# A Fourier stage on operands split in high and low parts, and attention loads on three semaphores

## The chip, the cores and the metric

The kernel runs on one core of a Trainium2 chip (the program uses no other). The metric is the time of the whole program on the device in microseconds (us), the median of several executions. The engines that compute are TensorE (PE in the rows; its weight loads are shown apart as PEld), VectorE (DVE), ScalarE (ACT) and GpSimd (POOL). SyncE (SP, its sequencer SPq) issues the DMAs.

## The reference

Two transformer-like layers follow each other on T = 2048 tokens of 1024 features. The first has five branches (spatial gating, forgetting attention, mLSTM, RWKV-7, attention over a memory of 256 tokens). The second has a Fourier branch and a neighbourhood attention. What the change touches:

```python
def _fourier(u, w_four):                      # u: 2048 x 512, four groups of 128 channels
    ug = u.reshape(b, l, F_GROUPS, F_GROUP_DIM)
    y = jnp.real(jnp.fft.fft2(ug, axes=(1, 3))) * ((l * F_GROUP_DIM) ** -0.5)
    return y.reshape(b, l, F_WIDTH) @ w_four

def forgetting_attention / memory_attention / _neighbourhood_attention:
    s = q @ k^T (+ decay or bias);  p = softmax(s);  o = p @ v
```

## The kernel before

The program is a row of phases; a barrier of all engines ends each. All tensors are float32. Most matrix products use operands kept as two `F32R` parts, high (the value rounded) and low (what the rounding left), and add three passes: high by high, high by low, low by high (`PASSES`). The Fourier phase is an exception: its matmuls take plain float32 operands.

**The Fourier phase** (`fourier`, between the feature pass 2 and the neighbourhood attention). The input `u` (4 blocks of 128 channels by 2049 columns) comes with five DMAs. The product of the channel transform `ch` and the weights `w4` gives `wcs` (8 products of 128x128 by 128x512, lines 2282, 2330, 2350). VectorE folds `u` by its symmetries into `fold[a % 2]`, four kinds `f` for each of four token blocks `a` (lines 2366 to 2381: eight operations a block). TensorE multiplies: 16 results of 4 products each (line 2294), which ScalarE (f = 0, 1) and VectorE (f = 2, 3) copy to `zz`. Two small results follow (`middle_row`, line 2300; `first_row`, lines 2307 and 2308). Then come 8 output groups `i`: 4 products for the cosines (line 2316), for the first four groups one more with a single row (`turns`, line 2319), 4 for the sines (line 2322). The tables `cs[i % 2]`, 512 KB a group, are loaded by SP (line 2247). ScalarE copies the sines out of PSUM (line 2344), VectorE forms their difference and sum with the cosines (2404, 2405), SP stores both (2262, 2265). All orders are written out by hand, engine by engine; table i + 2 is loaded when the sines of group i are done:

```python
            def load(i):
                if i >= 2:
                    sp.wait_ge(sin_ready, i - 1)
                sp.dma_start(cs[i % 2][:]..., d["dft_tokens"][i]).then_inc(cs_in[i % 2], 16)
```

**The attentions** (`attention`, used by `fox_attention`, `mem_attention` and `neighbourhood`). For each head, TensorE first computes units (line 1301: scores of a block of queries, of which VectorE takes the largest), then steps of `scores` (lines 1329 to 1337) and, two steps later, `values` (line 1346). The rows of a head come by `load_head` with 10, 7 or 11 DMAs, all counted on one semaphore `head_in`, for which TensorE waits once, before the head's first unit. `run_together` mixes the order of an attention with that of another stage by due times: `fox_attention` with the mLSTM (tiles `heads_...`), `mem_attention` with the RWKV factors (`mem_...`, `cells_...`), the neighbourhood attention (`nbr_...`) with the staging of the output weights. On each engine that order is fixed. POOL prepares constants (`const_ready`, line 1268) before the fox attention's first TensorE instruction (line 1496).

## Time and profile before

| what | value |
|---|---|
| median of 3 runs | 3731.46 us (3725.37 to 3754.88) |
| the profiled execution: time, span of its trace | 3737.91 us, 3736.2 us |
| mean granted TensorE clock, share of full speed | 0.914 |
| busy: PE, PEld, DVE, ACT, POOL | 87%, 67%, 39%, 24%, 21% |
| TensorE instructions of the span | 14595 matmuls, as many weight loads |
| Fourier phase in the trace | from 2963.2 us to about 3115 us |

A busy share is taken over the whole span, and the modelled ends of matmuls overlap, so that TensorE's speed is read from the starts of its instructions. A float32 product is two MATMUL rows in the trace, a pass on `F32R` operands one. Each phase has its own limit; what a change is worth is read where it lies.

### The profile page before, as it was taken

How to read it: one execution, taken by the hardware profiler on the slowest of the kernel's cores; microseconds unless marked ns; L12 is line 12 of the kernel's file. 1: busy time of each engine (PE TensorE's matmuls, PEld its weight loads, DVE VectorE, ACT ScalarE, POOL GpSimd, SP SyncE). 2: the span in 40 equal slices, each digit the busy share in tenths (PEclk: the TensorE clock that was granted, in tenths of full speed). 3: DMA queues.
4: the chain of work that ended last, by engine and by line, in shares of the span. 5: the costliest groups of instructions: out<-in, count | busy, mean ns of one | idle time of the engine just before them, and what ended most of it. 6: DMA issues, size and time to landing. Idle time of an engine off the chain costs nothing. (4 is left out here: it accounts for less than half of the span.)

```text
span 3736.2 us, 40044 instructions
## 1 busy us (share of the span) xinstructions
PE 3256.7 (87%) x14595; PEld 2496.7 (67%) x14595; DVE 1464.2 (39%) x2536; ACT 881.1 (24%) x1433; POOL 786.3 (21%) x843
## 2 busy tenths in 40 slices
PE   4949999899996988865699499799999895999799
PEld 2727888688885666543499388677888633666587
DVE  0023333313312667567544022277200122777533
ACT  1022221211011333342122133332001101544400
POOL 2043222211111212144333322111111001000121
PEclk7679999899997999966699699899999997999899
DMA  5333232412226134033100466522222217666364
GB/s 171 115 124 108 86 102 85 166 67 72 72 75 145 46 78 111 19 97 82 34 10 12 133 185 186 176 79 112 83 86 78 91 40 156 129 152 140 84 193 146
DMA packets 312454, 385.39 MB, mean 103 GB/s; under 512 B 86407, under 2 KB 244216, under 8 KB 297720
## 3 DMA queue, kind: packets, MB, share of 16 engines
q1 hardware_dynamic: 296276, 379.33, 35.5%
q10 hardware_dynamic: 16016, 3.95, 0.6%
q8 instruction: 95, 1.56, 0.2%
q14 instruction: 67, 0.55, 0.1%
HBM read 247.56 MB, written 135.66 MB: 103 GB/s over the span
## 5 line engine op out<-in xcount | busy, mean ns | idle before, releaser
L611 PE MATMUL f_psum_out<-f_x_high,f_w_high 128*128 128x512 f32 x1440 | 567.5, 394 | 33.3 <-DVE f_x_low L594 24.2
L611 PE MATMUL f_psum_out<-f_x_low,f_w_high 128*128 128x512 f32 x1440 | 563.2, 391 | 0.0
L611 PE MATMUL f_psum_out<-f_x_high,f_w_low 128*128 128x512 f32 x1440 | 562.8, 391 | 0.0
L611 PEld LDWEIGHTS f_psum_out<-f_x_high,f_w_high 128*128 128x128 f32 x1440 | 272.1, 189 | 94.0 <-issue 19.4
L611 PEld LDWEIGHTS f_psum_out<-f_x_low,f_w_high 128*128 128x128 f32 x1440 | 272.2, 189 | 57.4 <-issue 1.7
L611 PEld LDWEIGHTS f_psum_out<-f_x_high,f_w_low 128*128 128x128 f32 x1440 | 272.0, 189 | 57.2
L1346 PE MATMUL nbr_psum_o<-nbr_probT,nbr_v 128*128 128x512 f32 (+3 forms) x576 | 236.4, 491 | 0.3 <-ACT nbr_probT L1397 0.3
L481 PE MATMUL p_psum_proj<-p_w_high,p_h_high 128*128 128x512 f32 x512 | 208.3, 407 | 19.4 <-POOL p_w_low L296 10.5
L602 POOL CAST f_w_high<-f_w 128x1024 fp32r<-128x1024 f32 x45 | 46.7, 1039 | 768.3 <-PE f_psum_out L611 552.3
L481 PE MATMUL p_psum_proj<-p_w_low,p_h_high 128*128 128x512 f32 x512 | 202.5, 395 | 0.0
L481 PE MATMUL p_psum_proj<-p_w_high,p_h_low 128*128 128x512 f32 x512 | 202.1, 395 | 0.0
L1301 PE MATMUL nbr_psum_m<-nbr_kT,nbr_q_high 128*128 128x256 f32 (+3 forms) x352 | 158.8, 500 | 35.3 <-DMA nbr_v<-scratch_ctx_v 29.0
L1402 ACT ACTIVATE heads_probT<-heads_psum_s,heads_a_cols 128x512 f32<-128x512 f32 (+3 forms) x160 | 99.7, 623 | 276.7 <-PE heads_psum_s L1337 276.6
L1910 PE MATMUL p_psum_o<-p_w_high,p_mix_high 128*128 128x512 f32 x320 | 130.4, 408 | 26.0 <-POOL p_w_low L1979 24.8
L1346 PE MATMUL heads_psum_o<-heads_probT,heads_v 128*128 128x512 f32 (+3 forms) x320 | 148.1, 546 | 0.0
L1424 DVE CUSTOM_DVE_ANT_0 nbr_psum_m<-nbr_psum_m,nbr_inner_q 128x448 f32<-128x448 f32 x192 | 120.8, 631 | 63.9 <-PE nbr_psum_m L1301 62.9
L1397 ACT ACTIVATE nbr_probT<-nbr_probT 128x384 f32<-128x384 f32 (+2 forms) x224 | 108.6, 492 | 141.3 <-DVE nbr_probT L1440 140.5
L481 PEld LDWEIGHTS p_psum_proj<-p_w_high,p_h_high 128*128 128x128 f32 x512 | 97.8, 191 | 45.9 <-POOL p_w_low L296 12.3
L2158 DVE RECIPROCAL f_work<-f_work 128x2048 f32<-128x2048 f32 x8 | 103.6, 12952 | 62.2 <-ACT f_work L2131 62.2
L1910 PE MATMUL p_psum_o<-p_w_low,p_mix_high 128*128 128x512 f32 x320 | 127.5, 399 | 0.0
L1910 PE MATMUL p_psum_o<-p_w_high,p_mix_low 128*128 128x512 f32 x320 | 127.5, 398 | 0.0
L1301 PEld LDWEIGHTS nbr_psum_m<-nbr_kT,nbr_q_high 128*128 128x128 f32 x352 | 67.2, 196 | 81.6 <-issue 58.9
(547 smaller groups left out, 6220.5 us busy)
## 6 DMA issues: line engine op xcount, KB each, us to landing
f_w<-in_w_fm SPq DMA_DIRECT2D x45, 512.0 KB, 5.8
ada_w<-in_w_ada SPq DMA_DIRECT2D x6, 2048.0 KB, 17.6
scratch_qkmT<-p_qkT_out SPq DMA_DIRECT2D x32, 384.0 KB, 4.7
scratch_z1T<-f_out SPq DMA_DIRECT2D x10, 1024.0 KB, 4.8
p_z<-scratch_z1T SPq DMA_DIRECT2D x16, 640.0 KB, 5.8
p_xt<-in_x SPq DMA_DIRECT2D x16, 512.0 KB, 3.9
p_staging<-in_w_tok SPq DMA_DIRECT2D x8, 1024.0 KB, 5.7
scratch_hT<-p_h_slot SPq DMA_DIRECT2D x16, 512.0 KB
```

Source lines behind the costliest of these rows:

```text
L481: last = nc.tensor.matmul(p_proj[n][:], h_parts[i % 2][h_part][:, k, :], w_parts[w_part][:, k, n * BANK:(n + 1) * BANK], start=(k == 0 and ...
L602: nc.gpsimd.tensor_copy(self.w_parts[b][0][:], self.w[b][:])
L611: last = nc.tensor.matmul(self.p_out[b][:, at], self.w_parts[b][w_part][:, k, :], self.x_parts[x_part][:, k, at], start=(k == 0 and i == 0 ...
L1301: last = nc.tensor.matmul(out[:, at:at + n], query_rows(h % 2, q1[h % 2])[:, u * P:(u + 1) * P], key_rows(h % 2)[:, k:k + n], start=True, ...
L1346: nc.tensor.matmul(p_o[n % o_bufs][:, lo:hi], v[h % 2][:, b, :], probT[s % P_BUFS][:, lo:hi], start=first, stop=end).then_inc(o_ready, 1)
L1397: nc.scalar.activation(out, out, ACT.Exp).then_inc(prob_ready, 1)
L1402: nc.scalar.activation(out, p_s[s % s_bufs][:, lo:hi], ACT.Exp, bias=key_bias.column(h, b) if key_bias else 0.0).then_inc(prob_ready, 1)
L1424: last = nc.vector.tensor_tensor_reduce(scores, scores, table, 1.0, -3e38, ALU.add, ALU.max, top)
L1910: end = nc.tensor.matmul(p_o[:, n * BANK:(n + 1) * BANK], mix_parts[b][x_part][:, k, :], w_parts[w_part][:, k, n * BANK:(n + 1) * BANK], s ...
L2158: nc.vector.reciprocal(work[b][:], work[b][:])
```

## The change

Fourier phase: `wcs`, `fold`, `zz`, the tables, `middle`, `middle_row`, `turns` and `scale` become `F32R`, all but the last two in a high and a low part, and every product in the loops becomes three passes (`products`, `PASSES`); the 8 products that make `wcs` stay float32. For the splitting ScalarE now rounds (`high_of_w`, `high_of_fold`, `high_of_table`, the copies to `z_parts[0]`), and VectorE (for weights, z and the row) and POOL (for folds and tables) subtract. The split table of group i takes half of `fold[0]`; outputs and sines are placed in `u`. The reload of a raw table waits for its split. The first row of the output is computed after group 1. Attentions: the loads of a head are issued in the order of first use and counted on three semaphores, for which TensorE waits before the first unit, the first scores step and the first values step of the head.

```diff
-        def enter(h):
-            if h not in seen:
-                pe.wait_ge(head_in[h % 2], 16 * n_loads * (h // 2 + 1))
-                seen.append(h)
+        def await_loads(arrived, n, h):
+            if (n, h) not in seen:
+                pe.wait_ge(arrived[h % 2], 16 * loads[n] * (h // 2 + 1))
+                seen.append((n, h))
...
             h, q, u, pieces, masked = plan.units[plan.items[i][1]]
-            enter(h)
+            await_loads(tops_in, 0, h)
...
         def scores(s):
             h, q, b, lo, hi, first, _ = plan.steps[s]
             n, cols, out = plan.group(h, q), slice(q * BANK + lo, q * BANK + hi), p_s[s % s_bufs]
+            await_loads(scores_in, 1, h)
...
         def values(s):
             h, q, b, lo, hi, first, end = plan.steps[s]
             n = plan.group(h, q)
+            await_loads(values_in, 2, h)
...
             key_bias.load(sp, d["fox_a"])
+        sp.dma_start(raw(kx[b][0:HD, :]), d["qkmT"][0, GW + h * HD:GW + (h + 1) * HD, :]).then_inc(tops_in, 16)
+        sp.dma_start(raw(kx[b][HD:HD + 2, :]), d["fox_rows"][h]).then_inc(tops_in, 16)
+        sp.dma_start(raw(qx[b][0:HD, :]), d["qkmT"][0, h * HD:(h + 1) * HD, :]).then_inc(tops_in, 16)
         for part in range(2):
             sp.dma_start(raw(kT[b][part * HD:(part + 1) * HD, :]), d["qkmT"][part, GW + h * HD:GW + (h + 1) * HD, :])\
-                .then_inc(head_in, 16)
+                .then_inc(scores_in, 16)
             for q, half in ((q1, 0), (q2, 1)):
-                sp.dma_start(raw(q[part * HD:(part + 1) * HD, :]), d["qkmT"][half, h * HD:(h + 1) * HD, :]).then_inc(head_in, 16)
-        sp.dma_start(raw(kx[b][0:HD, :]), d["qkmT"][0, GW + h * HD:GW + (h + 1) * HD, :]).then_inc(head_in, 16)
-        sp.dma_start(raw(kx[b][HD:HD + 2, :]), d["fox_rows"][h]).then_inc(head_in, 16)
-        sp.dma_start(raw(qx[b][0:HD, :]), d["qkmT"][0, h * HD:(h + 1) * HD, :]).then_inc(head_in, 16)
+                sp.dma_start(raw(q[part * HD:(part + 1) * HD, :]), d["qkmT"][half, h * HD:(h + 1) * HD, :]).then_inc(scores_in, 16)
         sp.dma_start(v[b][:, :, b * HD:(b + 1) * HD], d["fox_v"].rearrange("(n p) c -> p n c", p=P)[:, :, h * HD:(h + 1) * HD])\
-            .then_inc(head_in, 16)
...
-    u, wcs = sb("u", [P, FK, T + 1]), sb("wcs", [P, 2, FK, D2])
...
+    u = sb("u", [P, FK, T + 1])
+    w_parts = [sb(f"w_{part}", [P, 2, FK, D2], F32R) for part in ("high", "low")]
...
-    middle, middle_row = sb("middle", [P, FK, 1]), sb("middle_row", [1, D2])
-    zz = sb("zz", [P, 4, NQ_T, D2])
-    cs = [sb(f"cs{b}", [P, NQ_T, 2, P]) for b in range(2)]
...
+    full = sb("full", [P, 4, FK, P])
+    fold = [sb(f"fold{b}", [P, 2, 4, FK, P], F32R) for b in range(2)]
...
+    row_parts = sb("row_parts", [1, 2, D2], F32R)
+    z_parts = [sb(f"z_{part}", [P, 4, NQ_T, D2], F32R) for part in ("high", "low")]
+    cs = [sb(f"cs{b}", [P, 2, NQ_T, P]) for b in range(RAWS)]
...
+    def table(i, part):
+
+        return fold[0][:, part, i % 2 * 2:i % 2 * 2 + 2]
...
             def load(i):
-                if i >= 2:
-                    sp.wait_ge(sin_ready, i - 1)
-                sp.dma_start(cs[i % 2][:].rearrange("p n s m -> p (n s m)"), d["dft_tokens"][i]).then_inc(cs_in[i % 2], 16)
-
...
+                if i >= RAWS:
+                    sp.wait_ge(table_low, i - RAWS + 1)
+                sp.dma_start(cs[i % RAWS][:].rearrange("p s n m -> p (s n m)"), d["dft_tokens"][i]).then_inc(cs_in[i % RAWS], 16)
...
+            for i in range(RAWS):
+                load(i)
...
-            sp.wait_ge(row_kept, 1)
-            sp.dma_start(d["y2"][0:1, :], first_row[:]).then_inc(row_stored, 16)
             for i, (parity, b) in enumerate(GROUPS_OUT):
-                if i + 2 < len(GROUPS_OUT):
-                    load(i + 2)
+                if i + RAWS < len(GROUPS_OUT):
+                    load(i + RAWS)
                 sp.wait_ge(out_ready, i + 1)
...
+                if i == 2:
+                    sp.wait_ge(row_kept, 1)
+                    sp.dma_start(d["y2"][0:1, :], first_row[:]).then_inc(row_stored, 16)
...
+            for n in range(HALVES):
+                a, odd = n // 2, n % 2
+                at = slice(2 * odd, 2 * odd + 2)
+                pool.wait_ge(fold_high, n + 1)
+                nc.gpsimd.tensor_tensor(fold[a % 2][:, 1, at], full[:, at], fold[a % 2][:, 0, at], ALU.subtract).then_inc(fold_low, 1)
+            for i in range(len(GROUPS_OUT)):
+                pool.wait_ge(table_high, i + 1)
+                if i >= 2:
+                    pool.wait_ge(sin_ready, i - 1)
+                nc.gpsimd.tensor_tensor(table(i, 1), cs[i % RAWS][:], table(i, 0), ALU.subtract).then_inc(table_low, 1)
...
+            over_k = [(s, m, k) for s, m in PASSES for k in range(FK)]
...
                     if f % 2 == 0:
-                        pe.wait_ge(even_ready if f == 0 else odd_ready, a + 1)
-                    if a == 0:
...
+                        pe.wait_ge(fold_low, 2 * a + f // 2 + 1)
...
-                    for k in range(FK):
-                        last = nc.tensor.matmul(p_b[a % 2 * 4 + f][:], fold[a % 2][:, f, k, :], wcs[:, f // 2, k, :],
-                                                start=(k == 0), stop=(k == FK - 1))
-                    last.then_inc(z_ready, 1)
...
+                        pe.wait_ge(z_low, 4 * (a - 2) + f + 1)
+                    products(p_b[a % 2 * 4 + f][:], over_k, lambda part, k: fold[a % 2][:, part, f, k, :],
+                             lambda part, k: w_parts[part][:, f // 2, k, :]).then_inc(z_ready, 1)
...
-                pe.wait_ge(cs_in[i % 2], 16 * (i // 2 + 1))
+                pe.wait_ge(table_low, i + 1)
...
+                if i == 0:
+                    pe.wait_ge(z_low, 4 * (NQ_T - 1) + 3)
...
+                if i == 1:
+                    pe.wait_ge(row_low, 1)
...
-                for a in range(NQ_T):
-                    last = nc.tensor.matmul(cosines[:], cs[i % 2][:, a, 0, :], zz[:, parity, a, :], start=(a == 0),
-                                            stop=(parity == 1 and a == NQ_T - 1))
+                last = products(cosines[:], over_k, lambda part, a: table(i, part)[:, 0, a, :],
+                                lambda part, a: z_parts[part][:, parity, a, :], more=parity == 0)
...
+                    for part in range(2):
+                        last = nc.tensor.matmul(cosines[:], turns[:], row_parts[:, part, :], start=False, stop=(part == 1))
...
+                products(of_sines[:], over_k, lambda part, a: table(i, part)[:, 1, a, :],
+                         lambda part, a: z_parts[part][:, 2 + parity, a, :]).then_inc(sin_ready, 1)
...
+            def high_of_w(i):
+                act.wait_ge(w_ready, i + 1)
+                for k in range(FK):
+                    nc.scalar.activation(w_parts[0][:, i, k, :], p_b[i * FK + k][:], ACT.Copy).then_inc(w_high, 1)
...
+                if a >= 2:
...
+                nc.scalar.activation(fold[a % 2][:, 0, at], full[:, at], ACT.Copy).then_inc(fold_high, 1)
+
+            def high_of_table(i):
+                act.wait_ge(cs_in[i % RAWS], 16 * (i // RAWS + 1))
+                if i >= 2:
...
+                nc.scalar.activation(table(i, 0), cs[i % RAWS][:], ACT.Copy).then_inc(table_high, 1)
+
+            high_of_w(0)
+            high_of_fold(0, 0)
+            high_of_w(1)
+            high_of_fold(0, 1)
...
-                for f in range(2):
+                if a + 1 < NQ_T:
+                    high_of_fold(a + 1, 0)
+                    high_of_fold(a + 1, 1)
+                for f in range(4):
...
-                    nc.scalar.activation(zz[:, f, a, :], p_b[a % 2 * 4 + f][:], ACT.Copy).then_inc(z_even_kept, 1)
+                    nc.scalar.activation(z_parts[0][:, f, a, :], p_b[a % 2 * 4 + f][:], ACT.Copy).then_inc(z_high, 1)
+                    if a == NQ_T - 1 and f < 2:
+                        high_of_table(f)
...
             for i in range(len(GROUPS_OUT)):
                 act.wait_ge(sin_ready, i + 1)
+                if i + 2 < len(GROUPS_OUT):
+                    high_of_table(i + 2)
...
-                nc.scalar.activation(sines[i % 2][:], p_b[2 + i % 2][:], ACT.Copy).then_inc(sines_kept, 1)
+                nc.scalar.activation(sines(i), p_b[2 + i % 2][:], ACT.Copy).then_inc(sines_kept, 1)
...
+            def low_of_w(i):
+                for k in range(FK):
+                    dve.wait_ge(w_high, FK * i + k + 1)
+                    last = nc.vector.tensor_tensor(w_parts[1][:, i, k, :], p_b[i * FK + k][:], w_parts[0][:, i, k, :], ALU.subtract)
+                last.then_inc(w_low, 1)
```

SP's queue in the Fourier phase of before, behind the first two table loads (`four_cs` a raw table, `scratch_y2<-` the stores of one group). Before:

```order
L2254 DMA scratch_y2<-four_first_row 1x512
L2247 DMA four_cs0<-in_dft_tokens 128x1024
L2262 DMA scratch_y2<-four_out0_0 128x512
L2265 DMA scratch_y2<-four_out0_1 64x512 x2
L2247 DMA four_cs1<-in_dft_tokens 128x1024
L2262 DMA scratch_y2<-four_out1_0 128x512
```

The same place of the changed kernel (`four_u` now holds the outputs):

```order
L2265 DMA four_cs0<-in_dft_tokens 128x1024
L2277 DMA scratch_y2<-four_u 128x512
L2280 DMA scratch_y2<-four_u 64x512 x2
L2265 DMA four_cs1<-in_dft_tokens 128x1024
L2277 DMA scratch_y2<-four_u 128x512
L2280 DMA scratch_y2<-four_u 64x512 x2
```

The alternation of loads and stores is the same; the first row has moved behind the third group's stores, and what each load waits for is another semaphore (in the diff).

ScalarE's queue in the output groups of the changed kernel, from its first reloaded table (`four_fold0<-` rounds a table, `four_u<-` copies the sines):

```order
L2388 ACTIVATE four_fold0<-four_cs0 128x1024
L2411 ACTIVATE four_u<-four_psum_b2 128x512
L2388 ACTIVATE four_fold0<-four_cs1 128x1024
L2411 ACTIVATE four_u<-four_psum_b3 128x512
L2414 ACTIVATE four_first_row<-four_psum_b7 1x512
L2388 ACTIVATE four_fold0<-four_cs0 128x1024
L2411 ACTIVATE four_u<-four_psum_b2 128x512
```

Before, the row was:

```order
L2344 ACTIVATE four_sines0<-four_psum_b2 128x512
L2344 ACTIVATE four_sines1<-four_psum_b3 128x512
L2344 ACTIVATE four_sines0<-four_psum_b2 128x512
L2344 ACTIVATE four_sines1<-four_psum_b3 128x512
L2344 ACTIVATE four_sines0<-four_psum_b2 128x512
```

So the rounding of the table of group i + 2 now stands ahead of the copy of the sines of group i.

SP's queue at the first head of the fox attention, before:

```order
L1527 DMA heads_kT0<-scratch_qkmT 64x2048
L1530 DMA heads_q_high0<-scratch_qkmT 64x2048
L1530 DMA heads_q_low0<-scratch_qkmT 64x2048
L1527 DMA heads_kT0<-scratch_qkmT 64x2048
L1530 DMA heads_q_high0<-scratch_qkmT 64x2048
L1530 DMA heads_q_low0<-scratch_qkmT 64x2048
L1531 DMA heads_kx0<-scratch_qkmT 64x2048
L1532 DMA heads_kx0<-scratch_fox_rows 2x2048
L1533 DMA heads_qx0<-scratch_qkmT 64x2048
L1534 DMA heads_v0<-scratch_fox_v 128x16x64
```

and in the changed kernel:

```order
L1528 DMA heads_kx0<-scratch_qkmT 64x2048
L1529 DMA heads_kx0<-scratch_fox_rows 2x2048
L1530 DMA heads_qx0<-scratch_qkmT 64x2048
L1532 DMA heads_kT0<-scratch_qkmT 64x2048
L1535 DMA heads_q_high0<-scratch_qkmT 64x2048
L1535 DMA heads_q_low0<-scratch_qkmT 64x2048
L1532 DMA heads_kT0<-scratch_qkmT 64x2048
L1535 DMA heads_q_high0<-scratch_qkmT 64x2048
L1535 DMA heads_q_low0<-scratch_qkmT 64x2048
L1536 DMA heads_v0<-scratch_fox_v 128x16x64
```

`kx` and `qx`, all that the units read, come first; `v` stays last.

## Rows read from the trace of the kernel before

**Rows 1.** Waits of TensorE: who waited for whom, us in total, times, longest.
```profile
PE four_psum_b L2316 <- DMA four_cs<-in_dft_tokens: 2.9, 1, 2.9
```

**Rows 2.** Timeline of TensorE, Fourier phase: start us, us, engine, line, tiles, count.
```profile
3035.43 3.59 PE L2300 MATMUL four_psum_b<-four_wcs,four_middle 128*1 128x512 f32 x8
...
3044.37 3.70 PE L2316 MATMUL four_psum_b<-four_zz,four_cs 128*128 128x512 f32 x8
...
3076.93 3.60 PE L2316 MATMUL four_psum_b<-four_zz,four_cs 128*128 128x512 f32 x8
3080.37 3.60 PE L2322 MATMUL four_psum_b<-four_zz,four_cs 128*128 128x512 f32 x8
...
3104.14 3.60 PE L2322 MATMUL four_psum_b<-four_zz,four_cs 128*128 128x512 f32 x8
```

**Rows 3.** The same view in feature pass 2; eleven more passes lie between these two.
```profile
2900.37 0.39 PE L611 MATMUL f_psum_out<-f_x_high,f_w_high 128*128 128x512 f32 x1
...
2903.09 0.39 PE L611 MATMUL f_psum_out<-f_x_high,f_w_high 128*128 128x512 f32 x1
```

**Rows 4.** Stretches: us, busy PE, PEld, DVE, ACT, POOL, granted clock, DMA share, GB/s.
```profile
2978.00:2984.00 6.00, 6.00 (x9) 2.40 (x9) 5.53 (x11) 0.00 (x0) 0.00 (x0) 0.57 0.03 11
...
3093.00:3108.00 15.00, 14.00 (x32) 6.00 (x32) 2.15 (x4) 0.82 (x2) 0.00 (x0) 1.00 0.31 91
```

**Rows 5.** Timeline of all engines at the start of the Fourier phase.
```profile
2968.34 2.06 ACT L2330 ACTIVATE four_wcs<-four_psum_b 128x512 f32<-128x512 f32 x4 [12.18 <-PE four_psum_b L2282]
...
2974.45 0.69 DVE L2366 TENSOR_TENSOR four_sum<-four_u 128x512 f32<-128x512 f32 x1 [0.19 <-issue]
...
2977.53 57.97 PE L2294 MATMUL four_psum_b<-four_wcs,four_fold 128*128 128x512 f32 x128 [5.79 <-DVEq L2375]
```

**Rows 6.** Groups of instructions by shape: busy us, mean ns of one, idle before.
```profile
L2680 POOL TENSOR_TENSOR fin_mix_low<-fin_mix,fin_mix_high 128x1024 fp32r<-128x1024 f32 x16 | 38.2, 2388 | 149.1 <-ACT fin_mix_high L2669 149.1
L2669 ACT ACTIVATE fin_mix_high<-fin_mix 128x1024 fp32r<-128x1024 f32 x16 | 17.0, 1060 | 160.9 <-DVE fin_mix L2696 160.9
```

**Rows 7.** Timeline of ScalarE, VectorE and SP's queue around group 1 of the outputs.
```profile
3060.90 0.60 ACT L2344 ACTIVATE four_sines<-four_psum_b 128x512 f32<-128x512 f32 x1 [7.52 <-PE four_psum_b L2322]
3061.60 0.69 DVE L2404 TENSOR_TENSOR four_out<-four_psum_b,four_sines 128x512 f32<-128x512 f32 x1 [6.83 <-ACT four_sines L2344]
...
3063.34 1.38 SPq L2265 DMA_DIRECT2D scratch_y<-four_out  x2
```

**Rows 8.** Tile `four_cs`, time to landing: all eight loads, then loads 6 and 7 alone.
```profile
DMA to landing us min/median/max: 3.2/4.3/11.6
...
DMA to landing us min/median/max: 9.3/9.3/9.3
...
DMA to landing us min/median/max: 5.4/5.4/5.4
```

**Rows 9.** Timeline of TensorE at the first head of the fox attention.
```profile
1178.94 0.34 PE L1496 MATMUL heads_psum_o<-ident,heads_a_rows 64*128 64x64 f32 x1 [4.15 <-POOLq L1268]
...
1188.30 0.45 PE L1301 MATMUL heads_psum_m<-heads_kx,heads_qx 66*128 66x128 f32 x1 [9.02 <-DMA heads_v<-scratch_fox_v]
...
1199.45 1.91 PE L1346 MATMUL heads_psum_o<-heads_probT,heads_v 128*128 128x512 f32 x2
```

**Rows 10.** Stretches, columns as in rows 4: the rest of that phase, and the factors phase.
```profile
1230.00:1580.00 350.00, 314.05 (x1455) 221.60 (x1453) 236.02 (x514) 121.60 (x205) 74.11 (x90) 0.98 0.28 65
1650.00:1800.00 150.00, 94.61 (x293) 59.12 (x293) 118.53 (x221) 37.34 (x92) 77.75 (x96) 0.71 0.26 56
```

**Rows 11.** Waits of VectorE (columns as in rows 1), and its timeline after 1752 us.
```profile
DVE nbr_psum_m L1424 <- DMA nbr_edge_k<-scratch_rel_tableT: 41.0, 7, 33.7
...
1752.12 0.36 DVE L2771 TENSOR_TENSOR mem_cells_less<-mem_cells_low,mem_cells_x 128x192 f32<-128x192 f32 x1
...
1753.22 0.70 DVE L2771 TENSOR_TENSOR mem_cells_less<-mem_cells_low,mem_cells_x 128x207 f32<-128x207 f32 x1
...
1766.66 0.76 DVE L1426 TENSOR_REDUCE mem_tops<-mem_psum_m 128x1 f32<-128x256 f32 x2 [2.07 <-PE mem_psum_m L1301]
```

More of the change, by code:

```diff
@@ L2318, in _ @@
                 if parity == 0:
-                    last = nc.tensor.matmul(cosines[:], turns[:], middle_row[:], start=False, stop=True)
-                last.then_inc(cos_ready, 1)
-                for a in range(NQ_T):
-                    last = nc.tensor.matmul(of_sines[:], cs[i % 2][:, a, 1, :], zz[:, 2 + parity, a, :], start=(a == 0),
-                                            stop=(a == NQ_T - 1))
-                last.then_inc(sin_ready, 1)
+                    if i == 0:
+                        pe.wait_ge(scaled, 1)
+                        pe.wait_ge(row_low, 1)
@@ L2360, in folds @@
                 dve.wait_ge(half_in[a // 2], 16 * (3 - a // 2))
-                if a >= 2:
-                    dve.wait_ge(z_ready, 4 * (a - 1))
                 if a == 2:
-                    nc.vector.tensor_tensor(middle[:], one(QUARTER), one(3 * QUARTER), ALU.add).then_inc(middle_ready, 1)
-                to = fold[a % 2]
-                nc.vector.tensor_tensor(sums[0][:], near[0], far[0], ALU.add)
-                nc.vector.tensor_tensor(sums[1][:], far[1], near[1], ALU.add)
+                    for n in range(2):
+                        nc.vector.tensor_tensor(middle[:, :, n:n + 1], one(QUARTER), one(3 * QUARTER), ALU.add)
@@ L3964 @@
         "dft_channels": np.stack([np.cos(angle_c), np.sin(angle_c)], axis=1).astype(np.float32),
[L3965 removed]
+        "dft_tokens": waves.reshape(PARITIES * NQ_T, P, 2 * NQ_T * P).astype(np.float32),
         "dft_turns": turns.reshape(1, P).astype(np.float32),
```

212 lines of the change are left out of this document (120 added, 92 removed).

## The prediction

> **What bounds the kernel now.** I read the waits first: TensorE, the busiest engine, waits for loads that this change touches in the Fourier phase [rows 1] and at the start of the fox attention [rows 9]. Then the timeline of the Fourier phase [rows 2], where TensorE runs nearly without a gap: its instructions set the phase's length, and the reader should look at the distance of starts, not at the durations. Four products (eight MATMUL rows) take 3080.37 - 3076.93 = 3.44 us, so one float32 product takes 0.86 us. In the feature pass before it, twelve passes on rounded operands of the same 128x128 by 128x512 shape take 2903.09 - 2900.37 = 2.72 us, 0.227 us each [rows 3]. Three passes are 0.68 us against 0.86: a gain of 0.18 us a product, if nothing else is late.
>
> **The change, part by part. Fourier, first half.** At the phase's start the clock is low: granted 0.57 from 2978 to 2984, and 1.00 late in the phase [rows 4]. The low stretch follows the 5.79 us for which TensorE had waited [rows 5]. The 64 products of line 2294 run from 2977.53 to 3035.43, 57.9 us [rows 2, 5]; 64 x 0.86 = 55.0, the rest, 2.8 to 2.9 us, is the low clock. After: 192 x 0.227 = 43.6, with the same 2.8 (the same kind of gap lies ahead) 46.4 us.
> The first fold must now also be split. ScalarE rounds the first four weight blocks from 2968.34 to 2970.4 as before [rows 5]; VectorE, which copied the other four, now subtracts the first four, each as it comes, at 0.69 us or less, until about 2971.5; the input halves land about then. Fold even takes from 2974.45 to 2977.5 now, 3.05 us, so it ends near 2975.0; then rounding of 128x1024 on ScalarE, 1.06, and the subtraction on POOL, 2.39 [rows 6], with 0.2 for handing over: TensorE starts at about 2978.8, 1.3 us later than now.
> In each of the four rounds VectorE has eight operations of 0.61 to 0.69 us and four subtractions out of PSUM at 0.69 [rows 7], 7.7 us; ScalarE two roundings (2.1) and four copies (2.4); POOL two subtractions (4.8). TensorE's round takes 48 x 0.227 = 10.9 us, and covers all three; without this cover the price would be VectorE's excess. Round a + 1's even fold is ready some 7.5 us after round a begins.
> Then `middle`: 12 passes, 2.7 us. Its row is split while TensorE does the 12 cosine passes of group 0. The sum of scaled rows moves behind group 1 (10 passes, 2.3). So group 0 starts at 2978.8 + 46.4 + 2.7 = 3027.9 instead of 3044.37 [rows 2]: **16.5 us** earlier.
>
> **Fourier, output groups.** TensorE alone would need 24 x 0.227 = 5.44 us a group, 5.9 in the first four, and 2.3 for the row: 47.7 us in all, where it now needs 3104.14 + 3.5 - 3044.37 = 63.3. But read the code as a loop over three queues. SP issues load i + 3 only after the stores of group i. These wait for the sums, and these for the sines, whose copy on ScalarE now stands behind the rounding of table i + 2, which waits for load i + 2 to land. So load i + 3 is issued a full turn after load i + 2: d to land, 1.06 to round, then from the copy's start to the last store issued 3064.72 - 3060.90 = 3.82 us [rows 7] (the rounding is in [rows 6]), 0.1 to 0.2 for handing over: d + 5.0. That is above 5.44 for any d over 0.4 us. It was not so before, since a load there waited for the sines alone and ScalarE for no load. From group 0's start: its products end at 6.0; round, copy, sum, store, and load 3 is issued at 11.1. Loads 4 to 7 follow at distances of d + 5.0 (0.3 once more for the first row's store). Load 7 lands d later, is rounded and subtracted (3.7 with handing over), and group 7 takes 5.5. Sum: 11.1 + 4(d + 5.0) + 0.3 + d + 3.7 + 5.5 = 40.6 + 5d.
> What is d? The loads took 3.2 us at least; loads 6 and 7, issued just behind stores, took 9.3 and 5.4, and the longest, issued with the input, 11.6 [rows 8]. In the changed kernel each load is issued right behind 512 KB of stores, but these were begun 1.8 us ahead: near the low end, and I take 3.8. The phase part is 40.6 + 19 = 59.6 us against 63.3: **3.7 us** less. Bounds: d = 3.2 gives 6.7 less, d = 5.4 gives 4.3 more.
> The tail after the last group (sines, sum, stores, barrier) stays.
>
> **Attention loads.** Fox: the units need only `kx` and `qx`, now the first three loads; all DMAs are the same. TensorE must first do the transpose at 1178.94, for which POOL's constants are awaited, and can start units at about 1179.8 instead of 1188.30 [rows 9], 8.5 us earlier. The low parts and `kT` (six loads) have then to be in 4.7 us later, at 1184.5; they come ahead of `v`, which was the last to land at 1188.3, so at most 1 us is lost. `v` is wanted 11.15 us behind the first unit [rows 9], at 1190.9: in. The rest of this phase keeps TensorE busy for 314 of 350 us [rows 10], so the lead lasts: **8 us** (6 to 8.5).
> Memory: units can start some loads earlier too. But this phase keeps TensorE busy for 95 of 150 us and VectorE for 119 [rows 10]; where head 3's units come late, VectorE's gap is 2.07 us [rows 11]: **1 us** (0 to 4, two such places). Neighbourhood: TensorE can start earlier, but VectorE waits 33.7 us for `nbr_edge_k` [rows 11], issued behind all of the head's loads as before, and TensorE has three banks to fill: 0.
>
> Sum: 16.5 + 3.7 + 8 + 1 = 29.2 us. The profiled execution took 3737.9, so it would be 3708.7; the median of the three runs shown is 6.5 us lower, and against it I forecast 3731.5 - 29.2 = **3702 us**.
>
> **What pages say.** A float32 product took 0.86/0.227 = 3.8 times a rounded pass [rows 2, 3]. The Trainium skill, "FP8 and Floating Point Precision", section TensorE Precision Notes, counts true FP32 as four passes (high and low by high and low). By it three passes would cost 0.75 of a product, 0.645 us, and not 0.68, and the first half would gain another 2 us; I go by the rows.
>
> **The rivals.**
> *The loads are hidden after all* (an order of events that I misread, or very short landings): the outputs take 47.7 us, 11.9 less than forecast, in all 41 us less, 3690. For it: only the code's order speaks for the loop, no row of before shows it. Chance 0.10.
> *The clock falls while TensorE waits for tables.* It would idle 3 us a group in four groups. For it: granted 0.57 after a wait of 5.79 us [rows 4, 5] and 0.71 in the phase that is 63% busy [rows 10]. Against it: 1.00 after the single 2.9 us wait [rows 1, 4]. At half speed a group takes 10.9 us and groups 3 to 7 give 59.6 + 15.8 = 75.4: 3718. Chance 0.13.
> *Fox gives nothing*: the start is early but another load or the mLSTM's chain takes it back. Against it: rows 10. 3710. Chance 0.12.
> *VectorE slows beside POOL.* A subtraction of two SBUF operands took 0.36 us for 192 columns and 0.70 for 207 [rows 11], with POOL in the same work. If all eight folds double (4.9 to 9.8 us), VectorE's round is 12.6 us against 10.9: 1.7 x 3 = 5 us, 3707. The Trainium skill, "GPSIMD Engine Reference", says that POOL's SBUF interfaces are shared with VectorE, with contention where the latter has two SBUF inputs; these rows agree. But POOL works in 4.8 us of each round only, so that I expect 2 us more for VectorE, still covered. Chance 0.07 that it binds.
> *The loop of loads turns the gain*: every load lands as slowly as the slowest row, 11.6 us [rows 8]. The outputs take 40.6 + 58 = 98.6, 39 more than forecast: 3741, slower than before. It decides from d = 9.6 on (40.6 + 5d = 63.3 + 25.5), just above load 6's 9.3; slower by 1% would need d = 17. Against it: that load was issued with the whole input ahead of it. Chance 0.04.
> My forecast, with d from 3.2 to 5.4: 0.54, its own range 3696 to 3713.
>
> **How the numbers follow.** About 1%, 37 us, is what a measurement of this kernel can tell from no change; the runs shown lie 29 us apart. Faster by over 1% (below 3694) are the hidden loads and the edge of the forecast: 0.12. Slower by over 1% (above 3769) is only the tail of the last rival: 0.02. Within 1%: 0.86. The range for 8 in 10 takes in the hidden loads (3690) and the low clock (3718), and leaves out the slower case: 3688 to 3719.
>
> **What the profile after would show.** In the first half, starts of passes 0.227 us apart without gaps and group 0 some 49 us behind the first fold product; a gap at a round's start would show VectorE or POOL as the limit. In the outputs, loads 4 to 7 at distances of 8.5 to 9 us, ScalarE's rounding waiting for a DMA, TensorE waiting about 3 us for POOL's split before groups 4 to 7, at granted 1.00. If the groups stand 5.44 us apart, the loop was misread; if their passes stand 0.45 apart, the clock fell. In the fox phase, the first unit near 1180 counted from the same phase start, and all the phase's end some 8 us earlier. The neighbourhood phase should keep its length from first load to VectorE's first operation, 28 us. What would make the forecast wrong most is d.

## The result, and the profile after

The changed kernel takes 3726.2 us (median of 20 runs, 3710.9 to 3731.6), the kernel before 3735.2 (20 runs, 3725.3 to 3754.9). The ratio is 0.9963 with a 95% interval of 0.9949 to 0.9977: about 14 us less, between 9 and 19. (The two medians alone are 9.0 us apart, at the low edge of this.) So the kernel is a little faster, clear of noise, but by less than the bound of 1%. The forecast was 29.2 less, 3702 us, with a range from 3688 to 3719; the time lies above it, 24.2 us over the forecast. Of these 3.7 us are the base: the forecast subtracted from the median of three runs, 3731.5, where twenty give 3735.2. The rest, 15 us by the ratio and 20 by the medians, is gain that did not come.

The profiled execution of the changed kernel took 3728.2 us, its span is 3726.3 against 3736.2, mean granted clock 0.911. The barrier that ends each phase (line 84) gives each phase's length. Beside the two first traces the table has those of the experiments below, one trace a kernel and thirteen in all. "Old form" means one semaphore in that attention (or the Fourier stage of before), "new form" three semaphores (or the changed Fourier stage); kernels with a further edit in that very phase are left out. "Forecast" and "measured change" compare new with old.

| phase | before | after | all kernels with the old form | all with the new form | forecast | measured change |
|---|---|---|---|---|---|---|
| fox with mLSTM | 431.5 | 429.2 | 431.5 to 436.5, mean 434.1 (4) | 425.2 to 433.5, mean 428.7 (9) | -8 | -5.4, give or take 3 |
| memory | 235.0 | 233.6 | mean 235.1 (3) | mean 233.5 (10) | -1 | -1.6 |
| RWKV (not touched) | 242.1 | 239.2 | 229.5 to 242.7 in all 13 | | 0 | up to 13 either way, not by the edit |
| Fourier | 152.1 | 141.1 | 152.1, 154.7 | 141.1 to 142.6 (5) | -20.2 | -11 to -12 |
| neighbourhood | 410.6 | 419.1 | 410.6, 414.1, 416.5 | 409.3 to 419.1, mean 412.6 (7) | 0 | none clear (-1) |

The "give or take" is an estimate from the spread of the traces; one new trace (433.5) lies among the old ones. So two terms fell short: the Fourier phase by 9 us, and the fox phase by 2 to 3, which the spread does not quite prove. The 8.5 us more in the neighbourhood phase of this one trace are no effect of the change (experiments 1 to 3).

The Fourier phase in four stretches: to the first fold product, to output group 0, to the last copy of sines, to the barrier (columns: stretch, its length, busy time of each engine with its instructions, granted clock, mean busy share of the 16 DMA engines, GB/s).

```profile
2956.40:2973.00 16.60, 10.01 (x16) 4.04 (x16) 8.91 (x13) 5.07 (x9) 3.16 (x4) 0.71 0.86 316
2973.00:3021.60 48.60, 48.21 (x204) 38.02 (x205) 36.61 (x51) 17.45 (x25) 21.80 (x9) 0.97 0.04 12
3021.60:3089.70 68.10, 54.58 (x211) 39.26 (x209) 9.70 (x15) 10.92 (x15) 14.24 (x6) 0.90 0.31 93
3089.70:3097.50 7.80, 0.00 (x1) 0.00 (x0) 1.29 (x2) 0.60 (x1) 0.00 (x0) 0.65 0.24 67
```

The first half (48.6 us for 46.4 + 2.7 forecast) is as forecast: group 0 starts 65.2 us behind the phase's start where it was 81.2. The outputs should have taken 59.6 us and take 68.1, with TensorE busy for 54.6 of them. The waits (us in total, times, longest) show that 10.2 of 13.5 us are a single one, for the split of table 6 (tables, loads and groups are numbered 0 to 7):

```profile
PE four_psum_b L2311 <- POOL four_fold L2305: 13.5, 3, 10.2
```

SP's row in the same place (start, time the issue took, instruction):

```profile
3050.89 0.36 SPq L2265 DMA_DIRECT2D four_cs<-in_dft_tokens  x1
3057.44 0.25 SPq L2277 DMA_DIRECT2D scratch_y<-four_u  x1
3057.73 4.93 SPq L2280 DMA_DIRECT2D scratch_y<-four_u  x2
3062.71 0.59 SPq L2265 DMA_DIRECT2D four_cs<-in_dft_tokens  x1
3074.95 0.34 SPq L2277 DMA_DIRECT2D scratch_y<-four_u  x1
```

Line 2277 is the direct store of a group, line 2280 its two mirrored stores, line 2265 a table load. Behind the direct store of group 3 at 3057.44 the next issue is held (4.93 us for a pair that takes 1.12 elsewhere, 3.8 us more), and the load issued at 3062.71, load 6, lands 9.2 us later; loads 3, 4 and 5 took 4.7, 3.6 and 3.5. The DMA share in this place (columns as above):

```profile
3059.00:3061.00 2.00, 2.00 (x6) 1.60 (x5) 0.00 (x0) 0.00 (x0) 0.00 (x0) 0.50 0.06 15
3063.00:3065.00 2.00, 2.00 (x11) 1.55 (x9) 0.00 (x0) 0.00 (x0) 0.00 (x0) 1.00 0.86 219
3065.00:3067.00 2.00, 0.36 (x2) 0.00 (x0) 0.00 (x0) 0.00 (x0) 0.00 (x0) 1.00 0.45 173
3067.00:3069.00 2.00, 0.00 (x0) 0.00 (x0) 0.00 (x0) 0.00 (x0) 0.00 (x0) 0.78 0.07 26
3069.00:3071.00 2.00, 0.00 (x0) 0.00 (x0) 0.00 (x0) 0.00 (x0) 0.00 (x0) 0.50 0.07 27
```

0.06 to 0.07 is one busy engine of 16. The trace's single transfers show what load 6 waits for: 120 of its 128 rows of 4 KB move between 3063 and 3067, and the last eight, a sixteenth of the load, only after 3070, when the rows of the store are through. The direct store of group 3 is the only one with `rows = P - 1`, 127 rows instead of 128. The kernel before had the same two things at the same place: two mirrored stores in 4.92 us, and load 6 in 9.3 [rows 8]. The Trainium skill, "DMA: Bandwidth & Descriptors", section "Why a DMA increments its semaphore by 16 and not by 1", says that a transfer is split over the largest number of engines up to 16 that divides its slowest dimension on both sides, and gives 127 partitions as a case that runs on one. By that rule, the trace agrees.

### The profile page after: what moved, and what is told of

Read it like the earlier page. It is cut to its first block and busy times, and to the rows that moved or that the text cites. A ratio compares the mean times of both kernels' runs of the same rounds, so it can differ in the third digit from the quotient of the medians.

```text
span 3726.3 us, 40402 instructions
## 1 busy us (share of the span) xinstructions
PE 3246.1 (87%) x14727; PEld 2527.9 (68%) x14727; DVE 1480.8 (40%) x2552; ACT 902.5 (24%) x1461; POOL 827.0 (22%) x860
## 5 line engine op out<-in xcount | busy, mean ns | idle before, releaser
L1426 DVE CUSTOM_DVE_ANT_0 nbr_psum_m<-nbr_psum_m,nbr_inner_q 128x448 f32<-128x448 f32 x192 | 120.9, 631 | 66.2 <-PE nbr_psum_m L1301 65.2
```

Of the source, the lines that this page charges most:

```text
L1426: last = nc.vector.tensor_tensor_reduce(scores, scores, table, 1.0, -3e38, ALU.add, ALU.max, top)
```

## The experiments

All kernels below change the changed kernel or the kernel before, as said. Each ratio compares with runs of the kernel before on the same chip. Experiments 1, 2, 4 and 6 ran on one chip, 3, 5, 8 and 9 on a second, 7, 10 and 11 on a third, so that medians from different groups are compared only roughly.

**1. Attention loads alone** (the kernel before, with `attention` and the three `load_head` of the changed one), **and 2. Fourier stage alone** (the reverse).

> The kernel before with the three semaphores and the new load order in the three attentions, and the old Fourier stage. Theory A (the loads' gain is mostly given back inside the fox phase, by a wait for the low parts of q and by low clock after short waits): the phase with fox and mLSTM takes 429 us instead of 431.5, the memory phase 233.5 instead of 235, the Fourier phase 152 as before; in all 2 to 5 us less than before. Theory B (the forecast's own terms hold, and the changed kernel lost them elsewhere): 8 us less in the fox phase, 9 in all. On the neighbourhood phase, 8.5 us longer in the changed kernel's trace: if the three semaphores lengthen it, it takes about 419 us here too; if it is a matter of landing times and clock that differ between executions, it can be anywhere from 410 to 420 and will not follow the edit.

> The changed Fourier stage alone, attentions as before with one semaphore a head. The Fourier phase takes 141 us instead of 152 (that is the trace of the changed kernel), fox phase 431.5. Total about 11 us less than before. If the neighbourhood's 8.5 us come from the attention loads, that phase is back at 410.6; if they come from what the Fourier stage leaves behind (table layout in memory, or the state of the queues), it stays at 419; if from differences between executions, neither.

Measured: 0.9968 (0.9947 to 0.9988) and 0.9964 (0.9946 to 0.9983), 12 and 13 us less, with intervals of 8 and 7 either way: too wide to tell the theories apart by the total. Phases: fox 425.2 and 433.0, Fourier 154.7 and 141.6, neighbourhood 409.3 and 414.1. The Fourier phase is where theory A has it, give or take 3 us (154.7 for 152 in the old form). In the first kernel the fox phase gained 6.3 us, more than A expected; only the mean over all kernels (5.4, give or take 3) says how large that term is. In the neighbourhood phase neither value follows the edit: three semaphores gave the shortest of the kernels with the tables in their old place.

**3. The changed kernel once more.**

> The changed kernel itself once more. Theory A (the neighbourhood phase differs from execution to execution by landing times of the bias tables at the heads' boundaries and by short stretches at half clock behind such waits, 409 to 415 us in the four kernels run so far, whichever loads they have; 419.1 was the far end): 410 to 416 us here, and Fourier phase 141 and memory phase 233.5 to 234 as before. Theory B (419 belongs to this kernel): 418 to 420 again. Total 3720 to 3730.

Measured: 0.9954 (0.9933 to 0.9975), 3721.5 us; neighbourhood phase 412.3, Fourier 141.9, fox 425.7. Theory A. What differs in the neighbourhood phase are the heads' boundaries, where VectorE waits for the bias tables, and TensorE's clock behind them:

```profile
3214.94 0.70 DVE L1426 CUSTOM_DVE_ANT_0 nbr_psum_m<-nbr_psum_m,nbr_edge_q 128x512 f32<-128x512 f32 x1 [2.66 <-DMA nbr_edge_k<-scratch_rel_tableT]
```

```profile
3218.30:3221.70 3.40, 3.40 (x11) 2.35 (x9) 1.26 (x4) 1.56 (x4) 0.00 (x0) 0.50 0.07 16
3222.00:3226.00 4.00, 4.00 (x21) 3.17 (x21) 3.31 (x12) 1.05 (x2) 0.21 (x1) 1.00 0.01 3
```

VectorE's wait of 2.66 us for a table holds TensorE up, and behind it TensorE works at granted 0.50 for 3.4 us (11 matmuls, where a stretch of 4 us at 1.00 just behind has 21). At the next boundary the last table landed 7.1 us after its issue in this trace, and after 5.2, 5.5, 6.1, 6.0 us in those of the kernel before and of experiments 1, 3 and 4; at the one after that it took 7.8 in this trace and in experiment 3 alike.
These two things account for the differences. VectorE's waits for the tables sum to 46.3 us in this trace and 41.0 in that of before, and TensorE stood at granted 0.50 for 53.9 and 45.4 us of the phase, which costs at most half of that time. An estimate that takes both off, length less waits less half of the time at 0.50, leaves 345.9 and 346.9, and 345.5 to 348.4 in all ten traces with the tables in their old place, whose lengths go from 409.3 to 419.1. So the 8.5 us are waits for tables and low clock; no run shows what makes a table land later in one execution.

**4. The store of 127 rows in two parts.**

```diff
-                sp.dma_start(y2[parity, first:first + rows], out(i, 0)[0:rows, :]).then_inc(stored[i % 2], 16)
+                sp.dma_start(y2[parity, first:first + (rows if rows == P else 112)], out(i, 0)[0:(rows if rows == P else 112), :]).then_inc(stored[i % 2], 16)
+                if rows < P:
+                    sp.dma_start(y2[parity, first + 112:first + rows], out(i, 0)[112:rows, :]).then_inc(stored[1], 16)
...
```

(Two waits on `stored` count the extra store; they are left out here.)

> The changed kernel with one store edited: the 127 rows of group 3 are stored as 112 and 15 rows. Theory A (a transfer of 127 rows goes through one of the 16 DMA engines: while it runs the trace shows a DMA share of 0.06 to 0.07, SP's next issue is held for 4.3 us and the table load behind it lands after 9.2 instead of 3.6 us, which the loop of loads cannot hide): no held issue, load 6 lands in 3.5 to 4 us, TensorE's wait of 10.2 us before group 6 falls to about 3, and the Fourier phase takes 130 to 132 us instead of 141; total 10 us less than the changed kernel. Theory B (the held issue is a full queue after the many transfers of groups 0 to 3, whatever their shape): unchanged, 141.

Measured: 0.9919 (0.9891 to 0.9947), 3708.9 us; Fourier phase 132.8. SP's row and TensorE's wait:

```profile
3057.60 0.33 SPq L2277 DMA_DIRECT2D scratch_y<-four_u  x1
3057.97 0.44 SPq L2279 DMA_DIRECT2D scratch_y<-four_u  x1
3058.45 1.12 SPq L2282 DMA_DIRECT2D scratch_y<-four_u  x2
3059.62 0.58 SPq L2265 DMA_DIRECT2D four_cs<-in_dft_tokens  x1
```

```profile
PE four_psum_b L2313 <- POOL four_fold L2307: 5.8, 3, 2.3
```

No issue is held, load 6 lands in 3.6 us, and the outputs take 59.2 us; the forecast's loop gave 59.6. Theory A, with the phase 0.8 us over its range. The other traces agree: load 6 took 9.2 to 9.3 us in each of the eight kernels that keep the 127-row store (before and changed, old form and new), and 3.3 to 3.7 in the five that split it. The small store of 15 rows (3057.97) costs 0.44 us of issue.

**5. The same split in the kernel before.**

> The kernel before with only the 127-row store of group 3 split into 112 and 15 rows. Theory A: the held issue of 4.3 us goes and load 6 lands in 3.2 to 3.6 us instead of 9.3, but the loads there are issued a group ahead, and TensorE had waited only once, 2.9 us: the Fourier phase takes 149 us instead of 152, total 0 to 3 us less. Theory B (the shape of the store is not what holds the queue): issue and landing as before, 152.

Measured: 0.9978 (0.9957 to 0.9999); Fourier phase 149.3 instead of 152.1, load 6 in 3.3 us instead of 9.3, all sines copies from group 3 on 6.9 us apart. Theory A. So by these pairs of traces the same slow store cost the kernel before 2.8 us and the changed one 8.4 (the other traces of the unsplit forms, 154.7 and up to 142.6, would give 5.3 and 9.9): before, a load was issued a group ahead of its use; in the changed kernel it stands in the loop.

**6. The loop cut: sines copied out before the next table is rounded** (with the split store).

```diff
                 act.wait_ge(sin_ready, i + 1)
-                if i + 2 < len(GROUPS_OUT):
-                    high_of_table(i + 2)
                 if i >= 2:
                     act.wait_ge(out_ready, i - 1)
                 nc.scalar.activation(sines(i), p_b[2 + i % 2][:], ACT.Copy).then_inc(sines_kept, 1)
+                if i + 2 < len(GROUPS_OUT):
+                    high_of_table(i + 2)
```

> The changed kernel with the split store and one order changed on ScalarE: the sines of group i are copied out before the rounding of table i + 2, not behind it. Theory A (the turn of a group is the loop load, round, copy, sums, stores, next load, d + 5.0 us): the loop is cut, the next load is issued 3.8 us after the products instead of a whole landing later, table i + 3 is split 11.4 us after group i, so that a turn is 5.7 us; from group 0's start to the last copy of sines about 48 us instead of 68.1, Fourier phase 121 to 123 us, total 19 us less than the changed kernel. Theory B (the turns of 8.2 to 9.3 us are set by something else, such as POOL's 2.4 us subtraction or the half clock after each wait): at most 2 us less than with the split store alone.

Measured: 0.9902 (0.9876 to 0.9929), 3705.0 us; Fourier phase 124.5, 8.3 less than with the split alone. ScalarE, and the output stretch:

```profile
3050.33 0.60 ACT L2411 ACTIVATE four_u<-four_psum_b 128x512 f32<-128x512 f32 x1 [4.91 <-PE four_psum_b L2313]
3051.45 1.06 ACT L2390 ACTIVATE four_fold<-four_cs 128x1024 fp32r<-128x1024 f32 x1 [0.52 <-DMA four_cs<-in_dft_tokens]
3055.93 0.60 ACT L2411 ACTIVATE four_u<-four_psum_b 128x512 f32<-128x512 f32 x1 [3.42 <-PE four_psum_b L2313]
```

```profile
3021.70:3073.00 51.30, 51.26 (x211) 37.31 (x209) 9.70 (x15) 11.40 (x15) 14.36 (x6) 1.00 0.42 123
```

The copy (line 2411) now waits for TensorE and not for a DMA, groups stand 5.6 us apart, TensorE is busy for 51.26 of 51.3 us at granted 1.00. So TensorE's own instructions now set the length, and theory A holds. The phase is 1.5 us over the range expected since the first four groups take 6.46 us each where the others take 5.60: their two passes with a single row (`turns`) each add 0.43 us, not the 0.23 that the forecast took.

**7. The folds' low parts on VectorE instead of POOL** (`fold_low` is made by `nc.vector.tensor_tensor` behind each fold; POOL keeps the tables).

> The changed kernel with the eight subtractions that give the low parts of the folds moved from POOL to VectorE. It measures the disputed cost of POOL beside VectorE: in the changed kernel the first subtraction of an odd fold (128x512, both operands in SBUF) takes 2.7 us, four of them 10.9 us, as long as POOL's own subtraction runs beside it. Theory A (VectorE's operation waits out POOL's): it takes 0.7 us here, VectorE's round is about 10.5 us and still under TensorE's 10.9, the first fold product comes 1.3 us earlier (15.5 instead of 16.7 to 17.4 us behind the phase's start), and the phase is 1 to 1.5 us shorter than 141.8. Theory B (the 2.7 us are VectorE's own time for this form of operand): it stays 2.7 us, VectorE's round takes over 12 us and the phase is some 3 us longer.

Measured: Fourier phase 139.8 against 141.1 to 142.6; the first fold product comes 15.3 us behind the phase's start, where theory A has 15.5; ratio 0.9932 (0.9909 to 0.9956). By form (line, engine, operation, shapes, count | busy us, mean ns), first the changed kernel, VectorE and POOL:

```profile
L2462 DVE TENSOR_TENSOR four_full<-four_difference 128x512 f32<-128x512 f32 x4 | 10.9, 2713 | 0.3
L2442 DVE TENSOR_TENSOR four_sum<-four_u 128x512 f32<-128x512 f32 x4 | 3.7, 920 | 0.0
L2300 POOL TENSOR_TENSOR four_fold<-four_full,four_fold 128x1024 fp32r<-128x1024 f32 x8 | 19.6, 2444 | 22.8 <-ACT four_fold L2380 22.8
```

Then this kernel, VectorE alone:

```profile
L2457 DVE TENSOR_TENSOR four_full<-four_difference 128x512 f32<-128x512 f32 x4 | 2.8, 693 | 0.3
L2469 DVE TENSOR_TENSOR four_fold<-four_full,four_fold 128x1024 fp32r<-128x1024 f32 x8 | 9.5, 1222 | 1.5 <-ACT four_fold L2375 1.2
```

Line 2462 of the changed kernel is line 2457 here: the same subtraction of two SBUF operands takes 2713 ns while POOL subtracts, and 693 ns when it does not. POOL needs 2444 ns for 128x1024, VectorE 1222. One pair in the changed kernel (start, us):

```profile
2970.39 2.52 POOL L2300 TENSOR_TENSOR four_fold<-four_full,four_fold 128x1024 fp32r<-128x1024 f32 x1 [0.23 <-ACT four_fold L2380]
2970.78 2.67 DVE L2462 TENSOR_TENSOR four_full<-four_difference 128x512 f32<-128x512 f32 x1
```

VectorE's instruction ends 0.54 us after POOL's, less than what it needs alone; so do the four others of this phase that start beside a POOL instruction with both operands in SBUF (0.55 each). Theory A: VectorE waits POOL's instruction out. Its subtractions out of PSUM in the same phase (line 2482, 684 ns each, four of them from 2986.89 on beside a POOL instruction at 2986.45) are not slowed. The Trainium skill, "Trainium Architecture — The Big Picture", section "What this means for kernel authors", calls the port that the two share an exclusive lock and no split of bandwidth. By that statement, the rows agree.

**8. Fox on one semaphore** (the changed kernel, `fox_attention` with its old order and one semaphore).

> The changed kernel with the fox attention's loads in the old order on one semaphore; memory and neighbourhood attention keep three. Theory A (fox's lead of 8.6 us is 6.3 to 7 after 39 us of the phase and is partly spent on half clock later, leaving about 4): the fox phase takes 431 to 433 us against 428 to 430 of the changed kernel in this job, total 3 to 6 us more than the changed kernel. Theory B (fox gives nothing in the end): no difference. Theory C (the forecast's 8 us): 8 us more.

Measured: 0.9973 (0.9959 to 0.9986) beside 0.9954 for the changed kernel in the same group; fox phase 435.3 against 425.7. The medians differ by 7.8 us, but their intervals overlap. By this pair alone (9.6 us in the phase) theory C, 8 us, is nearer than A, both of whose ranges are missed; over all traces the three semaphores give 5.4 us, between A's 4 and C's 8, so that B is out and A and C are not told apart. TensorE's first unit comes 23.1 us behind the phase's start instead of 31.6, a lead of 8.6 us. Where its rest goes, in the changed kernel:

```profile
1179.01 0.47 PE L1301 MATMUL heads_psum_m<-heads_kx,heads_qx 66*128 66x128 f32 x1 [0.39 <-DVE heads_a_cols L1503]
1185.78 0.79 PE L1330 MATMUL heads_psum_s<-heads_q_high,heads_kT 128*128 128x512 f32 x1 [1.82 <-DMA heads_q_low<-scratch_qkmT]
```

The first scores wait 1.8 us for the last low part, the mLSTM's first product 1.0 for `heads_rows`. 39 us into the phase the lead is 6.3 to 7.0 us in the four traces with new loads that were compared there. It then shrinks where the clock falls to half for a moment. The same three stretches of the phase, first the changed kernel, then that of experiment 1 (columns as above):

```profile
1356.00:1366.00 10.00, 9.89 (x33) 6.29 (x34) 5.26 (x12) 3.34 (x6) 1.83 (x3) 0.83 0.20 55
1404.00:1414.00 10.00, 8.78 (x29) 6.59 (x30) 7.15 (x15) 1.27 (x2) 0.62 (x1) 0.66 1.01 208
1456.00:1461.00 5.00, 4.89 (x12) 2.77 (x12) 3.50 (x8) 1.37 (x2) 0.61 (x1) 0.66 0.38 108
```

```profile
1354.40:1364.40 10.00, 9.89 (x42) 6.48 (x42) 5.50 (x13) 4.15 (x7) 1.83 (x3) 1.00 0.24 68
1402.40:1412.40 10.00, 8.63 (x40) 5.95 (x39) 7.94 (x17) 2.83 (x6) 2.83 (x4) 1.00 1.05 202
1454.40:1459.40 5.00, 5.00 (x19) 3.16 (x18) 4.12 (x5) 2.44 (x5) 2.35 (x2) 1.00 0.24 62
```

TensorE was busy in both; in the first the lead over the kernel before fell from 6.0 to 4.3, from 4.3 to 3.8 and from 3.8 to 2.1 across them, in the second it stayed at 6.1 to 5.9. Whether new loads make such falls more frequent is open: the kernels differ by as much among themselves.

**9. Bias tables ahead of low parts and values** in the neighbourhood attention.

```diff
+        tables.load(sp, h, b)
         sp.dma_start(raw(q2[0:HD, :]), d["qk2T"][1, h * HD:(h + 1) * HD, :]).then_inc(scores_in, 16)
```

(the call behind `load_head` goes).

> The changed kernel with the bias tables of a neighbourhood head loaded before its low parts and values, not behind them. VectorE waits for the last of these tables (34 us from the phase before to the first operation 28.7 us behind the phase's start; 2 to 7 us at each later head's boundary) while TensorE has been let in at 13.7 us and stands behind it. Theory A (the tables are what the phase's start waits for): VectorE's first operation comes at 16 to 20 us instead of 28.7, the heads' boundaries lose their waits, and the phase takes 398 to 406 us instead of 410 to 419. Theory B (the wait goes on to the next loads in the row, low parts and values, which now land later): less than 3 us.

Measured: 0.9906 (0.9883 to 0.9928), 3709.3 us; neighbourhood phase 397.5. VectorE's waits in that phase (engine, line, waited for: us in total, times, longest), changed kernel and this one:

```profile
DVE nbr_psum_m L1426 <- DMA nbr_edge_k<-scratch_rel_tableT: 46.3, 7, 34.4
```

```profile
DVE nbr_psum_m L1424 <- DMA nbr_edge_k<-scratch_rel_tableT: 26.6, 1, 26.6
```

The first operation comes 20.8 us behind the phase's start instead of 28.7, and the six later waits are gone. Theory A, a little beyond its ranges on both sides (20.8 for 16 to 20, 397.5 for 398 to 406); the gain (15 us against the mean of the seven others, 12 to 22 against each) is as large as the whole change's.

**10, 11. All together**: split store, sines first, tables first; and the same with the folds' low parts on VectorE.

> The changed kernel with three edits together: split store, sines copied ahead of the rounding, neighbourhood tables loaded ahead of low parts and values. If the gains add: Fourier phase 124.5, neighbourhood phase 397.5 instead of 413, total about 8.4 + 8.3 + 15 = 32 us less than the changed kernel, 3690 to 3696, ratio to the kernel before 0.985 to 0.990. If a gain is given back by the next wait, the total stays above 3702.

> best1 with the folds' low parts made on VectorE as well. If VectorE's round stays under TensorE's, 1 to 1.5 us less than best1 by the Fourier phase (123 to 123.5), not to be told apart in the total; if not, 3 us more.

Measured: 3688.6 us, 0.9862 (0.9838 to 0.9886), and 3688.7 us, 0.9867 (0.9843 to 0.9891); Fourier phase 125.5 and 123.1, neighbourhood 396.6 and 397.0. The gains add, for 32 us expected: 33 and 38 us less than the changed kernel's two medians (on other chips), and 50 less than the kernel before on the same chip. The slowest execution of either, 3690.2, is below the fastest of the changed kernel, 3707.6.

## Why the prediction was wrong

**The step that failed: the landing time of load 6, and the issue ahead of it.** The forecast set up the loop of the output groups, 40.6 + 5d, and put one d = 3.8 us into all five turns, with bounds of 3.2 and 5.4. It had the row that says otherwise, load 6 with 9.3 us [rows 8], and read it as a load "issued just behind stores"; in the changed kernel every load is, and four of five took 3.5 to 4.7. It also put the stores of every group at the time that they took in group 1, 3.82 us from the copy on, where those of group 3 take 3.8 us longer. What made load 6 slow was the form of one store ahead of it, which the code shows (`rows = P - 1`) and which is the same in both kernels. With that store split, the same formula holds: 59.2 measured, 59.6 forecast (the five loads then take 3.5 to 4.6, 3.8 in the mean). The store costs 3.8 us of held issue and 5.6 of landing on the loop (9.2 for 3.6), of which 8.9 us show in the outputs and 8.4 in the phase. With every load's own time, 24.7 us in sum, and the held issue the formula gives 69.1 us; measured are 68.1. So the mechanism was right and the size of its last turns was not. A known outlier in the very resource that a change puts on the path belongs in the sum at its own place, not in the rival in which every load is slow.

**Right.** *First half:* group 0 starts 16.0 us earlier for 16.5. The 64 products took 45.8 us for 46.4 at 0.68 us each. (The Trainium skill, "FP8 and Floating Point Precision", section TensorE Precision Notes, counts true FP32 as four passes; three would then cost 0.645 us, and the 64 products 44.1, an estimate. The rows decide for 0.68.) *Loop:* it exists and sets the turn; experiment 6 removes it and 8.3 us with it. *Hidden loads* were the wrong reading, as forecast. The rival's price was off: TensorE alone needs 51.3 us there and not 47.7 (5.60 us a group for 5.44, and `turns`). *Low clock in the outputs:* it came, granted 0.50 behind the waits of 2.2 and 10.2 us and 0.90 over the stretch, but TensorE was not the limit there; a small part. *Memory:* 1.6 us for 1. *Neighbourhood:* no gain from the semaphores that the traces show, since VectorE waits for the tables; experiment 9 shows that these waits were worth 15 us.

**Sizes off.** *Start of the phase:* the first fold product comes 2.3 us later, not 1.3; the eight float32 products ahead of it, which the change leaves alone, took 10.0 us (granted 0.71 in that stretch) instead of 8.5. But 8.5 stands in the first trace of before only: they took 9.4 to 10.2 in all twelve others, old form too. So this us is no effect of the change. *VectorE beside POOL:* 2.0 us more in each round, as expected, and covered but for one gap of 0.3 us; the rival did not bind. *Fox:* 5.4 us for 8, where 8 is at the edge of what the spread allows. "At most 1 us is lost" to the low parts was 1.8, 1.0 went to `heads_rows`. In the traces that lost more, the loss lies where the clock falls to half, which the forecast did not price; that this is the cause was not tested by a run.
Corrected: 16.0 - 4.7 for the outputs (68.1 against 63.4) - 0.3 for the end of the phase = 11.0 in the Fourier phase, and 5.4 + 1.6: 18 us. The measured 14 has 18 in its interval (9 to 19), and so has the second comparison (17, between 9 and 25). The 9.0 us between the medians are half of it, and the spans of the two first traces differ by 9.9: the three phases that gained are 14.7 us shorter and RWKV 2.9, but the neighbourhood phase is 8.5 longer, and the other phases make up 0.8.

## What to carry to other kernels

When a change moves transfers onto the path, give each its own landing time from the trace and explain every outlier by its own form and that of its neighbours in the queue, before taking a mean. A store of 127 rows on one of 16 DMA engines cost 3 to 5 us while loads ran a group ahead and 8 to 10 once the loads stood in the loop. And look at what the engine that finally ends a wait is waiting for: three semaphores let TensorE in 8 us earlier in the neighbourhood attention (13.6 us behind the phase's start for 21.5) for no gain that shows, while moving the tables ahead gained 15.

## What the runs showed of the hardware

**The clock rose at different moments in different executions, for 13 us.** The RWKV phase, touched by no edit, took 229.5 to 229.6 us in three of 13 traces, 239.2 in one and 242.1 to 242.7 in nine. The same stretch of that phase, changed kernel and that of experiment 8:

```profile
1818.80:1833.80 15.00, 5.55 (x24) 3.66 (x24) 11.98 (x13) 0.25 (x1) 9.21 (x27) 0.50 0.03 9
1833.80:1863.80 30.00, 29.53 (x177) 26.18 (x176) 8.32 (x18) 6.38 (x20) 5.33 (x18) 0.68 0.01 2
```

```profile
1825.20:1840.20 15.00, 5.59 (x25) 3.69 (x26) 11.99 (x13) 0.29 (x1) 9.23 (x27) 0.51 0.04 9
1840.20:1870.20 30.00, 28.94 (x241) 26.11 (x241) 11.95 (x26) 7.82 (x25) 5.94 (x18) 1.00 0.01 2
```

TensorE is busy for 29 of 30 us in both second rows, but at granted 0.68 and at 1.00 (177 and 241 matmuls): the rise to 1.00 came 34 and 15 us behind the phase's start, and 44 in the trace of before. Nothing here shows what decides it. In every set of eight or more executions of one kernel the time goes with the mean granted clock (correlation -0.82 to -0.92; 0.001 more clock goes with 2 to 3 us less), which is most of their spread (standard deviation 5 to 10 us); sets of five or six give anything from -0.08 to -0.97. A single pair of traces can differ by up to 13 us in a phase that nobody changed; the phase lengths of several kernels side by side told the terms apart better than the medians did.
**A slow transfer blocks its neighbours.** 254 KB in 127 rows made SP's next issue take 4.3 us instead of 0.5, and a 512 KB load behind it 9.2 us instead of 3.6.
**VectorE stands still until POOL's instruction ends** when both have two operands in SBUF: 2713 ns against 693. With an operand in PSUM it does not: 684 ns beside POOL.
